# A hybrid diffusion step on one core: ranks counted in the rounded format, rows turned one product later, and the first experts' splits placed sooner among the routing steps

## The reference, cut to what matters

```python
x = x + gate1 * ((g_conv * conv_out + g_att * att) @ w_out)
h2 = rms_norm(x, norm2) * (1 + scale2) + shift2
g_logits = t @ w_group + b_group          # 4 groups
g_idx = argmax(g_logits)                  # one group for each token
e_sel = (t @ w_expert + b_expert)[group g_idx]   # its 4 experts
top_v, top_i = top_k(softmax(e_sel), 2)
hid = silu(t @ w1) * (t @ w3) * comb      # 16 experts, 256 wide
y = hid @ w2
```

## Time and profile before

| what | us |
|---|---|
| median of 3 runs | 1015.06 (1009.6 to 1017.67) |
| profiled execution, its own time | 1016.93 |
| its span | 1015.1 |
| TensorE busy | 944.1 (93%) |
| VectorE busy | 735.8 (72%) |
| ScalarE busy | 502.0 (49%) |
| mean granted TensorE clock | 0.965 of full |

### The profile page before, as it was taken

The page is one execution under the profiler, slowest core; times in us unless marked ns, Lnnn a source line. Parts: engine busy times, 40 slices in busy tenths (PEclk is TensorE's granted clock), DMA queues, the critical chain, the costliest instruction groups (busy, mean ns, idle before and its releaser), DMA issues.

```text
span 1015.1 us, 15190 instructions
## 1 busy us (share of the span) xinstructions
PE 944.1 (93%) x5854; PEld 783.4 (77%) x5854; DVE 735.8 (72%) x1216; ACT 502.0 (49%) x712; POOL 63.4 (6%) x62
## 2 busy tenths in 40 slices
PE   4899999999999789999978999999889978999997
PEld 1697798867878778888866977997579966888886
DVE  4567788565854579978967687895648657997895
ACT  4342623275422267747744336324663236774772
POOL 1000000064000000000001000000810000000000
PEclk9999999999999579999997999999999978999999
DMA  9933477501645159949946434563123205994971
GB/s 374 357 146 138 177 297 278 235 1 43 240 174 208 57 209 342 388 170 342 373 166 249 166 130 183 197 242 125 43 84 125 83 18 191 352 373 187 337 285 62
DMA packets 29017, 206.71 MB, mean 204 GB/s; under 512 B 3408, under 2 KB 3440, under 8 KB 4240
## 3 DMA queue, kind: packets, MB, share of 16 engines
q1 hardware_dynamic: 28656, 204.81, 53.4%
q0 software_dynamic: 288, 0.92, 0.3%
HBM read 203.98 MB, written 1.74 MB: 203 GB/s over the span
## 4 chain that ended last, share of the span: by engine, by line
PE 80%; DVE 11%; ACT 5%; issue 2%; DMA 1%; POOL 1%; DVEq 0%; SPq 0%; ACTq 0%
PE ps L853 58%; PE ps L840 6%; PE ps L864 4%; PE ps L1253 3%; PE ps L831 2%; ACT w_hi L710 1%; PE ps L1006 1%; PE ps L1089 1%; DVE w_lo L716 1%; PE ps L1077 1%; DVE x L2234 1%; POOL probs L810 1%; DVE w_lo L721 1%; DVE rs L1734 1%; ACT kT L1507 1%
## 5 line engine op out<-in xcount | busy, mean ns | idle before, releaser
L721 DVE TENSOR_TENSOR w_lo<-ring,w_hi 128x2048 fp32r<-128x2048 f32 (+1 forms) x100 | 224.0, 2247 | 32.8 <-ACT w_hi L1609 32.3
L853 PE MATMUL ps<-h_hi,w_hi 128*128 128x384 f32 x576 | 199.0, 345 | 5.7 <-issue 2.4
L1609 ACT ACTIVATE w_hi<-ring 128x2048 fp32r<-128x2048 f32 x96 | 183.6, 1919 | 30.3 <-PE ps L853 30.3
L853 PE MATMUL ps<-h_lo,w_hi 128*128 128x384 f32 x576 | 194.2, 337 | 0.0
L853 PE MATMUL ps<-h_hi,w_lo 128*128 128x384 f32 x576 | 194.0, 337 | 0.0
L716 DVE TENSOR_TENSOR w_lo<-ring,w_hi 128x2048 fp32r<-128x2048 f32 x42 | 95.8, 2289 | 53.5 <-ACT w_hi L710 53.5
L853 PEld LDWEIGHTS ps<-h_hi,w_hi 128*128 128x128 f32 x576 | 108.5, 188 | 19.9 <-issue 12.4
L853 PE MATMUL ps<-w_hi,hg_hi 128*128 128x512 f32 x256 | 106.4, 416 | 7.4 <-DVE w_lo L721 7.3
L710 ACT ACTIVATE w_hi<-ring 128x2048 fp32r<-128x2048 f32 x44 | 83.7, 1912 | 56.9 <-DMA ring<-wpre 46.3
L853 PEld LDWEIGHTS ps<-h_hi,w_lo 128*128 128x128 f32 x576 | 108.7, 189 | 0.0
L853 PEld LDWEIGHTS ps<-h_lo,w_hi 128*128 128x128 f32 x576 | 108.7, 189 | 0.0
(11 more groups left out here) (268 smaller groups left out, 1455.6 us busy)
## 6 DMA issues: line engine op xcount, KB each, us to landing
ring<-wpre SPq DMA_DIRECT2D x96, 1024.0 KB, 6.3
ring<-wmoe SPq DMA_DIRECT2D x96, 1024.0 KB, 6.3
x<-x SPq DMA_DIRECT2D x1, 1536.0 KB, 7.5
x_out<-x SPq DMA_DIRECT2D x4, 384.0 KB, 2.3
par<-par_in POOLq DMA_DIRECT2D x2, 367.5 KB, 4.7
const<-const_in SPq DMA_DIRECT2D x1, 314.0 KB, 3.2
ckv_out<-ckvT POOLq DMA_DIRECT2D x2, 64.0 KB, 2.2
kr_out<-kr POOLq DMA_DIRECT2D x2, 16.0 KB, 2.3
```

Of the source, the lines that this page charges most:

```text
L721: return nc.vector.tensor_tensor(out, whole, leading.bitcast(F32), ALU.subtract)
L853: m = mm(out, a, b, start=(start and i == 0 and j == 0), stop=(stop and i == n - 1 and j == 2))
L1609: af(w_hi[m % MOE_PLACES], slot(moe_slot(l, m)), ACT.Copy).then_inc(split_hi, 1)
```

## The change

It has five parts. (1) Ranks: a tile `counting` holds `ones` and `tri` rounded to float32r (ScalarE copies it at c = 6 of the projection), the one-hots are written in float32r with a zero tile behind them, and four float32r products take the place of three float32 ones and of VectorE's three additions. (2) `rms_rows` is filled right behind the reciprocals, no longer behind the one-hots. (3) Rows of chunk c - 2 are turned behind product c (c = 2 to 6), and split one step later. (4) hi(1) stands ahead of quarters 2 and 3, and the exponentials behind them; lo(1) stands ahead of quarters 2 and 3. (5) lo(2) stands ahead of `weighed`.

```diff
-        if 1 <= c <= HROW_EARLY:
-            add("hrow", c - 1, "dve", 5 + (c - 1) % 2)
+        if 2 <= c < HROW_EARLY + 2:
+            add("hrow", c - 2, "dve", 5 + c % 2)
...
+        counting = place("counting", 2 * P, F32R, at=gates_at + 4 * 2 * TOK)
...
-        oh_g = v3(sm(TT * 4), TT)
-        oh_sum = v3(sm(TT * 4), TT)
+        oh_r = v3(place("oh_r", (TT + 1) * 4, F32R), TT + 1)
+        oh_g = oh_r[:, 0:TT, :].bitcast(F32)
...
-                    if 1 <= c <= HROW_EARLY:
-                        turn_rows(c - 1)
+                    if 2 <= c < HROW_EARLY + 2:
+                        turn_rows(c - 2)
...
-                n = TT * GROUPS
-                mm(out[:, 0:n], tri, oh_g.rearrange("p t g -> p (t g)"), start=True, stop=False)
-                mm(out[:, GROUPS:n], ones, oh_sum[:, 0:TT - 1, :].rearrange("p t g -> p (t g)"), start=False, stop=True)
-
-                mm(out[:, n:n + GROUPS], ones, oh_sum[:, TT - 1, :], start=True, stop=True).then_inc(psum_full, 1)
+                mm(out[:, 0:(TT + 1) * GROUPS], counting[:, P:2 * P], oh_r, start=True, stop=False)
+                for t in range(TT):
+                    n = TT - t
+                    m = mm(out[:, (t + 1) * GROUPS:(TT + 1) * GROUPS], counting[:, 0:P],
+                           oh_r[:, t:t + 1, :].broadcast_to([P, n, GROUPS]), start=False, stop=(t == TT - 1))
+                m.then_inc(psum_full, 1)
...
-                    if 2 <= c < HROW_EARLY + 2:
-                        rows_top(c - 2)
+                    if 3 <= c < HROW_EARLY + 3:
+                        rows_top(c - 3)
...
+                    if c == KD - 2:
+
+                        af(counting, const[:, C_ONE:C_ONE + 2 * P], ACT.Copy)
...
                     gathered(i0, 1)
+                    hi(1)
+                    gathered(i0, 2)
+                    gathered(i0, 3)
                     act.wait_ge(ex_in, act.snap(i0 + PAIRS))
                     af(exo, ex, ACT.Exp).then_inc(ex_out, PAIRS)
-                    gathered(i0, 2)
-                    gathered(i0, 3)
-                    hi(1)
                     hi(2)
...
+            mark(vs(oh_r[:, TT, :], const[:, 0:GROUPS], 0.0, None, ALU.mult))
...
-                    if 2 <= c < HROW_EARLY + 2:
-                        rows_rest(c - 2)
+                    if 3 <= c < HROW_EARLY + 3:
+                        rows_rest(c - 3)
...
                 mark(nc.vector.reciprocal(cwr[:, :, EPG], rms))
+                mark(vs(rms_flat, const[:, 0:TT * P], 0.0, None, ALU.mult))
+                dve.wait_ge(dve_order, count[0])
+                top = rms_rows.rearrange("p t (j n) -> p t j n", j=QUADS)
+                mark(copy(top[:, 0, :, 0:3:2], rms[:, 0:1].unsqueeze(2).broadcast_to([P, QUADS, 2])))
...
-                chain(one_hot(oh_g, g_lg, best))
-
-                chain(copy(oh_sum[:, 0, :], oh_g[:, 0, :]))
-                chain(vt(oh_sum[:, 1, :], oh_sum[:, 0, :], oh_g[:, 1, :], ALU.add))
-                vt(oh_sum[:, 2, :], oh_sum[:, 1, :], oh_g[:, 2, :], ALU.add).then_inc(onehot_ready, 1)
-                mark(vs(rms_flat, const[:, 0:TT * P], 0.0, None, ALU.mult))
+                one_hot(oh_r[:, 0:TT, :], g_lg, best).then_inc(onehot_ready, 1)
                 for c in range(HROW_EARLY, KD):
                     rows_rest(c)
...
+                dve.wait_ge(onehot_ready, l + 1)
                 wait_full(dve, l, "rank")
...
                     choose(i0)
+                    lo(1)
                     gathered(i0, 2)
                     gathered(i0, 3)
-                    lo(1)
                     weigh_experts(i0)
+                    lo(2)
                     weighed(i0)
-                    lo(2)
```

More of the change, by code:

```diff
@@ L43 @@
 LAT_W = QL + KVL + ROPE
-SMALL = 328
+SMALL = 296
 GROUPS, EPG = 4, 4
@@ L2078, in _ @@
                 mark(nc.vector.reciprocal(cwr[:, :, EPG], rms))
+                mark(vs(rms_flat, const[:, 0:TT * P], 0.0, None, ALU.mult))
+                dve.wait_ge(dve_order, count[0])
+                top = rms_rows.rearrange("p t (j n) -> p t j n", j=QUADS)
+                mark(copy(top[:, 0, :, 0:3:2], rms[:, 0:1].unsqueeze(2).broadcast_to([P, QUADS, 2])))
+                for t in range(1, TT):
+                    mark(copy(top[:, t, :, 3:6:2], rms[:, t:t + 1].unsqueeze(2).broadcast_to([P, QUADS, 2])))
+                dve.wait_ge(dve_order, count[0])
+                mark(lower(top[:, 0, :, 1], rms[:, 0:1].broadcast_to([P, QUADS]), top[:, 0, :, 0]))
+                mark(lower(top[:, 1:TT, :, 4], rms[:, 1:TT].unsqueeze(2).broadcast_to([P, TT - 1, QUADS]), top[:, 1:TT, :, 3]))
                 def b4(a):
```

## The result

Over 20 runs of each kernel, the median is 1010.3 us against 1012.9, which is 0.26% less. The mean is 1008.1 against 1013.0: 4.9 us or 0.48% less, and from the scatter of the runs the 95% interval of that difference is 1.7 to 8.1 us. The measured ratio is 0.9917 (95% interval 0.9888 to 0.9947), or 8.4 us. All ratios here compare fast runs alone, and so leave out nine of the changed kernel's 20 (those from 1012.4 to 1014.1), three of e10_after_again's 12, four of e12_few_busy's 12, one of e8_no_lead_busy's 12, and none of the kernel before. Forecast were 11.3 us, put down as 1005.0. So the change is faster by 3 to 8 us, depending on how those nine runs are counted. Sorted, the 20 runs lie between 996.6 and 1014.1, five of them under 1002. The profiled execution took 1008.3 us, its span 1006.5: 8.6 less than before.

The account below looks back on a forecast made before the run. TensorE was 80% of the chain, VectorE 11%, counting only there or where TensorE stood still. 1.0 + 1.6 + 2.8 + 4.6 + 2.9 - 1.6 = 11.3 us off 1016.93 gave 1005.6, put down as 1005.0; range 998 to 1013.

Parts of the forecast that it names:

- rival A: Layer 1's gathers at half clock like layer 0's: 2.0 us lost instead of 4.6 won, 1012.2 us; chance 0.24.
- B: Rival: layer 0's gathers regain full clock like layer 1's, 9.5 us won instead of 2.9, 999.0 us; chance 0.14.
- The projection: Layer 0: product 4 starts 1.5 us earlier, 1.0 left after costs; new TensorE gap 1.3; layer 1 nothing.
- the clock's fall: Layer 0's projection, behind the stall before product 4: half-clock stretch gone, 1.6 us won, bounds 0 and 1.7.
- Routing: One-hot to reading of the ranks: 1.4 us won per layer, 2.8 in two, bounds 1.4 and 2.8.
- First experts, cold: Gathers at half clock throughout: turn(0) 29.3 us behind their start; 2.9 us won in layer 0.
- Warm: First experts, gathers back at full clock early: turn(0) 22.7 us behind their start.
- The new gaps: TensorE waits some 2 us before turn(0) in both layers; one clock fall counted, 1.6 us lost, bounds 0 and 3.4.
- layer 1's 4.6: First experts, layer 1: VectorE's work back to back, turn(0) at 853.7 instead of 858.3, 4.6 us won.
- Rival C: First experts' new order delays what TensorE needs; their 7.5 us not won, 3.8 left, 1013.1 us; chance 0.08.
- D: Rival: clock drops at the gap before turn(0) and stays at half for 27 us per layer, 1031 us; chance 0.04.

Follow-up runs that it names:

- e10_after_again: The changed kernel run again, with nothing changed: median 1004.3 us, ratio 0.9882 of before.
- e12_few_busy: The changed kernel with 4 extra 384-column TensorE products, results unused, behind the rank products: 1010.8 us, 0.9928 of before.
- e8_no_lead_busy: The changed kernel with parts 4 and 5 undone, plus 12 extra unused 384-column products behind the rank products: 1006.2 us, 0.9936 of before.
- e6_rows_only: The kernel before with part 3 alone (rows turned and split one product later): 1011.6 us, one run.
- e7_float32_ranks: The changed kernel with three float32 rank products and VectorE's three additions again, early filling kept: 1002.6 us, one run.
- e4_no_lead: The changed kernel with parts 4 and 5 undone (first experts in the old order): 1010.2 us, 0.9977 of before.
- e2_after_busy: The changed kernel with 12 extra 384-column TensorE products, results unused, behind the rank products: 995.0 us, 0.9823 of before.
- e11_turn_busy: e2_after_busy with 14 more unused 256-column products ahead of turn(0) of a layer's first pair: 995.3 us, 0.9820 of before.
- e3_weights_later: The changed kernel with VectorE's copy of the gathered weights behind lo(3), not lo(2), in a layer's first pair: 1004.0 us, 0.9910 of before.

## Why the prediction was right, and where its sizes were off

*What is right and what isn't.* The median, 1010.3, lies in the range of 998 to 1013, and the faster side was right. That range is wide, because it takes in rivals A and B; the forecast's own range, 1002 to 1009, misses the median by 1.3. Of the 11.3 us forecast, the profiled execution shows 8.6, the ratio 8.4 and the mean of all runs 4.9. The closeness of 8.6 owes something to luck: the unit's earlier landing gave some 2 us that the sum doesn't have, and about the same was lost between the layers.

*The projection.* Product 4 came 1.6 earlier behind the split, as worked out (1.5), and the clock's fall went, worth 1.3 for 1.6. e6_rows_only shows both alone. TensorE stood still for 0.4 us, not 1.3; only in e7_float32_ranks, where the unit landed late, was it 1.4. The other 2 us of that phase are the unit's earlier landing.

*Routing.* 1.4 in layer 1, to the tenth. Layer 0 had 0.7, because its last two groups of logit products (L1199, L1202) ran at half clock and took 0.65 longer. With the same routing layer 0 took 10.6 us in e10_after_again and 11.0 in e4_no_lead (11.3 here), so this differs by execution. The float32r record at 0.21 was the right one of the bounds. The sum didn't see that the two halves lean on each other: with the filling alone, float32 ranks would have been late.

*First experts, cold.* 28.7, in both traces that had a cold layer, for a forecast of 29.3: 3.3 won, not 2.9. *Warm*: 22.7 and in e2_after_busy 21.2 and 22.0, for 22.7. VectorE's chain of work was the right thing to add up, and the 2 us gap of TensorE before turn(0) is there (2.21). In e2_after_busy VectorE needs 12.7 from choose to the gating in both layers and doesn't wait, as the sum has it; with gathers at half clock its wait for TensorE's weights comes on top.

*The new gaps.* One fall in two was counted; layer 0 had it (24 and 12 products in 9.70), layer 1 not. In the traces of the new order the gap is 2.21 in the five layers where VectorE waits for the weights, and the clock fell behind four of these gaps. It is 1.77 in ten layers where VectorE doesn't wait, and the clock never fell there. (Left out are e11_turn_busy, where the gap is filled, and layer 0 of e3_weights_later with 1.10, which had no fall either.) So a cold layer mostly pays twice, by its late weights and by the fall behind them, which the sum didn't see.

*The term that was mis-sized* is layer 1's 4.6. It took for granted that its gathers would be warm again, because they were in the one execution before. They came back only with the last quarter, and 1.8 was left. This goes half the way to rival A, to which I gave 0.24 with 4.7 us won at 1012.2: nine of the 20 runs lie within 1012.4 and 1014.1. An estimate from the rows fits them: the profiled 1008.3, with 3.2 more for a layer 1 at 28.7 and 1.5 for a fall behind its turn(0), is 1013.0. That these are the ones with both layers cold is likely but not shown, since none of them was profiled. The three traces of the changed kernel and its order (one cold and one late, one warm and one cold, both warm by force) give 1008.3, 1004.9 and 995.4 us, in the order of the model. Rival C, that the order does nothing, is refuted by the traces of e4_no_lead and by e8_no_lead_busy. Of D only the start was seen: the clock does fall behind the new gap, but it came back after 3.4 us each time.

## What to carry to other kernels

Before adding up what a moved instruction saves, sort the engine's own work and what it waits for: here the first experts were bound by VectorE's sum of work, in cold layers from TensorE's gathered weights on, and the sums gave the time of turn(0) within 1.5 us, warm and cold. Where a stage of dense products follows a standstill of TensorE, its time has two values; work out both, and don't take the one that a single profile happens to show. Twelve products with no use, in a gap that is idle anyway, brought the changed kernel from means of 1008.1 and 1004.9 us (20 and 12 runs) to 994.9 (6 runs). That is 10 to 13 us, more than the change itself; with the old order, in which VectorE was the bound, the same products were worth 3.

## What the runs showed of the hardware that was not expected

What TensorE did before a stretch bore on the clock that it was granted there, and a little work wasn't enough. After a standstill of 3.9 to 4.6 us the 256-column products of the gathers, back to back but for short breaks, stayed at 0.50 for all of their 15.0 us in seven of the 14 layers traced without extra products. In one they stayed so for 11.5 us, and in six the clock was back 3.4 to 4.3 us after their start; the changed kernel alone showed all three. What decides between these is open. With 12 products of 384 columns in the gap they ran at full clock by their second quarter in all twelve layers of the six kernels that had them; with 4, one layer took 12.0 us for its gathers and the other 10.4, instead of 8.7 to 9.4. And in the projection, TensorE stood still for 2.5 and 3.0 us in the two traces with the old order of rows, and the clock fell; in the twelve with the new one it stood still for 0.4 to 1.4 us, and the clock stayed up.
